# Attention scores from queries and keys stored as rounded halves, stacked to 128 rows

## The reference

```python
proj = rmsnorm(x) @ w_in          # q, k, v of group A and of group B, 512 columns each
# group A: 4 heads of differential attention; 2 parts of q and k with 64 channels, v with 128
qa = partial_rope(rmsnorm(qa), cos, sin);  ka = partial_rope(rmsnorm(ka), cos, sin)
s = einsum('bhcqd,bhckd->bhcqk', q, k) * scale           # rows of 128 queries, keys up to them
p = softmax(where(mask, s, -inf));  w = p[0] - lam * p[1];  o = w @ v
# group B: 8 heads of stick-breaking attention, 64 channels
z = einsum('bhqd,bhkd->bhqk', q, k) * scale
log_keep = where(mask, log_sigmoid(-z), 0);  suffix = reversed cumsum of log_keep
a = where(mask, exp(log_sigmoid(z) + suffix - log_keep), 0);  o = a @ v
```

## Time and profile before

| | us |
|---|---|
| median of 3 runs | 3598.82 (3597.29 to 3598.83) |
| the profiled execution | 3593.81 |
| its span, first to last instruction | 3592.0 |
| PE busy | 3372.0 (94%) |
| DVE busy | 2401.5 (67%) |
| POOL busy | 1655.2 (46%) |
| ACT busy | 1048.7 (29%) |

### The profile page before, as it was taken

One profiled execution on the slowest core, in us unless ns is written; L12 is line 12 of the kernel. 1 busy time (PEld: TensorE's weight loads), 2 busy tenths in 40 slices (PEclk: granted clock), 3 DMA queues, 4 the chain that ended last, 5 costly groups with the idle time before them and its releaser, 6 DMA issues. The chain is left out here.

```text
span 3592.0 us, 45109 instructions
## 1 busy us (share of the span) xinstructions
PE 3372.0 (94%) x17090; PEld 2942.4 (82%) x17090; DVE 2401.5 (67%) x4484; ACT 1048.7 (29%) x1158; POOL 1655.2 (46%) x847
## 2 busy tenths in 40 slices
PE   7998989998899999999999999995899999999998
PEld 5886656666788999999899989995688888888886
DVE  2401658883311788999999999996567666666665
ACT  3221336652211222333333333332112211221120
POOL 2420000001211356555445544565787777877773
PEclk9997877778999999999999999997999999999999
DMA  3132000003221367666666766788887778777874
GB/s 126 70 115 101 24 24 12 12 1 135 80 88 45 137 206 234 206 239 238 236 234 227 241 232 239 251 321 320 308 295 284 289 289 305 283 286 283 310 277 160
DMA packets 252449, 697.16 MB, mean 194 GB/s; under 512 B 20208, under 2 KB 86640, under 8 KB 245104
## 3 DMA queue, kind: packets, MB, share of 16 engines
q1 hardware_dynamic: 178544, 426.35, 33.6%
q0 software_dynamic: 73728, 268.47, 21.1%
HBM read 564.72 MB, written 130.02 MB: 193 GB/s over the span
## 5 line engine op out<-in xcount | busy, mean ns | idle before, releaser
L1150 PE MATMUL hid_ps<-side_hi,u_hi 128*128 128x384 f32 x2048 | 531.3, 340 | 19.8 <-POOL u_lo L836 10.5
L845 POOL DMA_INDIRECT found<-in_u,pick_u x232 | 330.3, 1424 | 425.0 <-DVE found L1081 389.9
L1878 PE MATMUL part<-v_hi,act_hi 128*128 128x512 f32 x1536 | 475.1, 391 | 50.6 <-POOL act_lo L1801 48.8
L1150 PE MATMUL hid_ps<-side_lo,u_hi 128*128 128x384 f32 x2048 | 522.5, 336 | 0.0
L1150 PE MATMUL hid_ps<-side_hi,u_lo 128*128 128x384 f32 x2048 | 522.5, 336 | 0.0
L1878 PE MATMUL part<-v_lo,act_hi 128*128 128x512 f32 x1536 | 474.2, 390 | 0.0
L1878 PE MATMUL part<-v_hi,act_lo 128*128 128x512 f32 x1536 | 473.7, 390 | 0.0
L836 POOL TENSOR_TENSOR u_lo<-u_raw,u_hi 128x1024 fp32r<-128x1024 f32 x128 | 327.5, 2559 | 264.4 <-ACT u_hi L795 263.8
L1817 DVE TENSOR_TENSOR acc<-acc,part 128x1024 f32<-128x1024 f32 x192 | 234.3, 1220 | 307.0 <-PE part L1878 306.9
L1150 PEld LDWEIGHTS hid_ps<-side_hi,u_hi 128*128 128x128 f32 x2048 | 366.8, 189 | 20.5 <-POOL u_lo L836 10.7
L1796 POOL TENSOR_TENSOR v_lo<-v_raw,v_hi 128x2048 fp32r<-128x2048 f32 x64 | 295.8, 4622 | 186.0 <-ACT v_hi L1769 185.4
(11 more groups left out here) (197 smaller groups left out, 5415.5 us busy)
## 6 DMA issues: line engine op xcount, KB each, us to landing
u_raw<-in_uT SPq DMA_DIRECT2D x128, 512.0 KB
v_raw<-in_v SPq DMA_DIRECT2D x64, 1024.0 KB
hid_d<-hid SPq DMA_DIRECT2D x128, 384.0 KB
gate_d<-stage SPq DMA_DIRECT2D x48, 1024.0 KB, 5.6
act_in<-hid_d SPq DMA_DIRECT2D x64, 768.0 KB, 7.6
gate_in<-gate_d SPq DMA_DIRECT2D x32, 1536.0 KB
w_raw<-in_w_in SPq DMA_DIRECT2D x6, 2048.0 KB, 8.3
w_raw<-in_wq SPq DMA_DIRECT2D x4, 2048.0 KB, 8.5
```

Source lines behind the costliest of these rows:

```text
L845: pool.indirect_dma_start(found[:, g], None, u_d, bass.IndirectOffsetOnAxis(ap=pick_u[:, g, n:n + 1], axis=0))\
L1150: mm = pe.matmul(hid_ps[:, s % 2, half, 0:W], w[:, s % 2, ch], x[:, ch, GB * P + half * W:GB * P + (half + 1) * W], start=n == 0, stop=n = ...
L1878: last = pe.matmul(part[:, n % BANKS, cols], a[:, s, j, rows], v[:, s, j, cols], start=j == 0 and m == 0, stop=j == J - 1 and m == 2)
```

## The change

The projection stores q and k as two rounded halves: ACT writes `st_hi` (fp32r), DVE writes `st_lo`, the PSUM value (scaled for q of B) less `st_hi`. Each has two slots; a slot is free when both stores of the use before have landed. v keeps `st` with two slots. The last transposes of q and of k, and the later items of PE, wait for the low halves too.

For each head or part, `attend` loads q's high half to rows 0 to 63 and its low half to rows 64 to 127 of `q_both`, and k's high half to both row halves of `k_hi`, its low half to both of `k_lo`: 12 transfers of 64 rows x 4 KB for a pair of heads, in place of two of 128 rows. A score call is then two fp32r matmuls over 128 rows, `q_both` by `k_hi` and `q_both` by `k_lo`, for each block of columns. In loop B the value matmul takes the 128 columns of both heads of the pair, and the rows of the other head are not read. `soft` and `logw` now share the memory of `prob`.

```diff
...
         sin = sb("sin", [P, TB, ROT])
         spare = sb("spare", [P, 4, TB // 2 * NH * ROT])
         sq = sb("sq", [P, 2, HALF])
-        st = sb("st", [P, 4, HALF])
+        st = sb("st", [P, 2, HALF])
+        st_hi = sb("st_hi", [P, 2, HALF], R)
+        st_lo = sb("st_lo", [P, 2, HALF], R)
         ss = sb("ss", [P, TB])
         rstd = sb("rstd", [P, TB])
         qk_ss = sb("qk_ss", [P, 2, TB, NH])
...
         rot_ok = sem("rot_ok")
         qt_ok = sem("qt_ok")
         st_ok = sem("st_ok")
-        st_out = [sem(f"st_out{n}") for n in range(4)]
+        st_lo_ok = sem("st_lo_ok")
+        v_out = [sem("v_out0"), sem("v_out1")]
+        qk_out = [sem("qk_out0"), sem("qk_out1")]
         block = c.enter_context(nc.Block())
...
             g, k = n // ITEMS, n % ITEMS
             return stores.index(({2: "va", 3: "qb", 4: "kb", 5: "vb"}[g], k)) + 1
+
+        def kind_index(n):
+
+            return sum((w[0] == "v") == (stores[n][0][0] == "v") for w, _ in stores[:n])
         @block.sync
         def _(sp):
...
             def store(n):
                 what, k = stores[n]
+                m = kind_index(n)
+                sp.wait_ge(st_ok, n + 1)
+                if what[0] == "v":
+                    cols = slice(0, HALF) if what == "va" else slice(HALF, D)
+                    sp.dma_start(v_d[k * P:(k + 1) * P, cols], st[:, m % 2]).then_inc(v_out[m % 2], 16)
+                    return
                 cols = slice((k % 2) * HALF, (k % 2) * HALF + HALF)
-                out = {"qa": qT_d[k // 2][:, cols], "ka": kT_d[k // 2][:, cols],
-                       "qb": qT_d[4 + k // 2][:, cols], "kb": kT_d[4 + k // 2][:, cols],
-                       "va": v_d[k * P:(k + 1) * P, 0:HALF], "vb": v_d[k * P:(k + 1) * P, HALF:D]}[what]
-                sp.wait_ge(st_ok, n + 1)
-                sp.dma_start(out, st[:, n % 4]).then_inc(st_out[n % 4], 16)
+                pair = k // 2 + (4 if what[1] == "b" else 0)
+                hi_d, lo_d = (q_hi_d, q_lo_d) if what[0] == "q" else (k_hi_d, k_lo_d)
+                sp.dma_start(hi_d[pair][:, cols], st_hi[:, m % 2].bitcast(F)).then_inc(qk_out[m % 2], 16)
+                sp.wait_ge(st_lo_ok, m + 1)
+                sp.dma_start(lo_d[pair][:, cols], st_lo[:, m % 2].bitcast(F)).then_inc(qk_out[m % 2], 16)
             load_x(0)
             sp.dma_start(gain[:, :], norm_g_d.unsqueeze(0).to_broadcast([P, D])).then_inc(small_in, 16)
...
                 if n == 3 * ITEMS + 5:
                     load_w(5)
                 store(n)
-            for n in range(4):
-                sp.wait_ge(st_out[n], 16 * len(stores) // 4)
+            for n in range(2):
+                sp.wait_ge(v_out[n], 16 * ITEMS)
+                sp.wait_ge(qk_out[n], 32 * 2 * ITEMS)
         @block.gpsimd
         def _(pool):
...
             def out_slot(n):
-                if n >= 4:
-                    act.wait_ge(st_out[n % 4], 16 * (n // 4))
-                return st[:, n % 4]
+                m = kind_index(n)
+                is_v = stores[n][0][0] == "v"
+                if m >= 2:
+                    act.wait_ge((v_out if is_v else qk_out)[m % 2], (16 if is_v else 32) * (m // 2))
+                return (st if is_v else st_hi)[:, m % 2]
             for tb in range(TB + 1):
                 if tb < TB:
...
                 if tb >= 1:
                     low(tb - 1)
             heads = "p b (h d) -> p b h d"
+
+            def store_low(n):
+                what, k = stores[n]
+                m = kind_index(n)
+                if what[1] == "a":
+                    src = tr_ps[:, k // 2 % 2, 4 * (k % 2):4 * (k % 2) + 4].rearrange("p a b -> p (a b)")
+                else:
+                    src = pr_ps[:, k % 4]
+                dve.wait_ge(st_ok, n + 1)
+                dve.scalar_tensor_tensor(out=st_lo[:, m % 2], in0=src, scalar=HD ** -0.5 if what == "qb" else 1.0,
+                                         in1=st_hi[:, m % 2].bitcast(F), op0=ALU.mult,
+                                         op1=ALU.subtract).then_inc(st_lo_ok, 1)
+
+            def store_lows(what):
+                for k in range(ITEMS):
+                    store_low(stores.index((what, k)))
+
             for g in range(2):
                 for k in range(ITEMS):
                     n = ITEMS * g + k
...
                                       ALU.add).then_inc(qss_ok, 1)
                 dve.wait_ge(qss_ok, ITEMS * (g + 1))
                 dve.tensor_scalar(qk_ss[:, g], qk_ss[:, g], 1.0 / HD, EPS, ALU.mult, ALU.add).then_inc(qvar_ok, 1)
+                if g == 1:
+                    store_lows("qa")
                 dve.wait_ge(qrstd_ok, g + 1)
                 flat = qk[:, g].rearrange("p b (h d) -> p (b h) d", d=HD)
                 dve.tensor_tensor(flat, flat, qk_rstd[:, g].rearrange("p b h -> p (b h)").unsqueeze(2)
...
                     dve.wait_ge(rot_mul, m + 1)
                     dve.tensor_tensor(q1, t[0], t[1], ALU.subtract)
                     dve.tensor_tensor(q2, t[2], t[3], ALU.add).then_inc(rot_ok, 1)
+            for what in ("ka", "qb", "kb"):
+                store_lows(what)
         @block.tensor
         def _(pe):
...
                     pe.wait_ge(copied, n - 3)
                 if n >= 4 + 2 * ITEMS:
                     pe.wait_ge(st_ok, stores_until(n - 4))
+                    if (n - 4) // ITEMS in (3, 4):
+                        pe.wait_ge(st_lo_ok, n - 4 - ITEMS + 1)
                 s = g % 2
                 if g in (3, 4):
                     wide = slice((k % 2) * HALF, (k % 2) * HALF + HALF)
...
                     pe.wait_ge(rot_ok, 2 * g)
                     for pair in range(4):
                         n = 4 * (g - 1) + pair
-                        if pair >= 2:
-                            pe.wait_ge(st_ok, STORED_BEFORE[g] + 2 * (pair - 1))
+                        if pair >= 2 or g == 2:
+                            pe.wait_ge(st_lo_ok, ITEMS * (g - 1) + 2 * (pair - 1))
                         for tb in range(TB):
                             last = pe.transpose(tr_ps[:, pair % 2, tb],
                                                 qk[:, g - 1, tb, pair * P:(pair + 1) * P], ident[:, :])
                         last.then_inc(qt_ok, 1)
-
-
-STORED_BEFORE = {1: 0, 2: 16}
 def route(nc, a_hi, a_lo, x_first, ident, x_d, w_out_d, norm_g_d, wq_d, keysT_d, h_d, score_d):
...
         mask_raw = sb("mask_raw", [P, 2, P])
         mask = sb("mask", [P, 2, P], R)
         unit = sb("unit", [P, P], R)
-        qT = sb("qT", [P, 2, T])
-        kT = sb("kT", [P, 2, T])
+        q_both = sb("q_both", [P, 4, T], R)
+        k_hi = sb("k_hi", [P, 4, T], R)
+        k_lo = sb("k_lo", [P, 4, T], R)
         v = sb("v", [P, TB, D])
         prob = sb("prob", [P, 3, 2, T])
-        soft = sb("soft", [P, 2, T])
-        logw = sb("logw", [P, 2, T])
+        soft = prob[:, 0]
+        logw = prob[:, 1]
         ones = sb("ones", [P, T])
         wT = sb("wT", [P, 4, PER, P])
         peak = sb("peak", [P, 4])
...
         @block.sync
         def _(sp):
             def load_pair(n):
-                sp.dma_start(qT[:, n % 2], qT_d[n]).then_inc(qk_in[n % 2], 16)
-                sp.dma_start(kT[:, n % 2], kT_d[n]).then_inc(qk_in[n % 2], 16)
+                for part in range(2):
+                    s = 2 * (n % 2) + part
+                    rows = slice(part * HD, part * HD + HD)
+                    for half, q_d in enumerate((q_hi_d, q_lo_d)):
+                        here = slice(half * HD, half * HD + HD)
+                        sp.dma_start(q_both[here, s].bitcast(F), q_d[n][rows]).then_inc(qk_in[n % 2], 16)
+                        sp.dma_start(k_hi[here, s].bitcast(F), k_hi_d[n][rows]).then_inc(qk_in[n % 2], 16)
+                        sp.dma_start(k_lo[here, s].bitcast(F), k_lo_d[n][rows]).then_inc(qk_in[n % 2], 16)
             load_pair(0)
             sp.dma_start(mask_raw[:, 0], mask_da_d).then_inc(mask_in, 16)
...
         @block.tensor
         def _(pe):
-            def scores(out, rows, buf, i, kind):
-
-                q = qT[rows, buf, i * P:(i + 1) * P]
+            LOADED = 16 * 12
+
+            def scores(out, s, i, kind):
+
+                q = q_both[:, s, i * P:(i + 1) * P]
                 for a, b in spans(i):
-                    pe.matmul(out[:, a:b], q, kT[rows, buf, a:b], start=True, stop=True)
-                pe.matmul(out[:, i * P:(i + 1) * P], q, kT[rows, buf, i * P:(i + 1) * P], start=True, stop=False)
+                    pe.matmul(out[:, a:b], q, k_hi[:, s, a:b], start=True, stop=False)
+                    pe.matmul(out[:, a:b], q, k_lo[:, s, a:b], start=False, stop=True)
+                d = slice(i * P, (i + 1) * P)
+                pe.matmul(out[:, d], q, k_hi[:, s, d], start=True, stop=False)
+                pe.matmul(out[:, d], q, k_lo[:, s, d], start=False, stop=False)
                 return pe.matmul(out[:, i * P:(i + 1) * P], unit[:, :], mask[:, kind], start=False, stop=True)
             def scores_a(u):
```

(15 more changed lines are left out.)

18 lines of the change are left out of this document (12 added, 6 removed).

## The result

The changed kernel takes 3540.15 us (median of 4 runs, 3538.07 to 3542.95) against 3598.06 (3595.53 to 3598.83) for the kernel before on the same chip: ratio 0.9841, 95% interval 0.9824 to 0.9858. Its profiled execution took 3538.5 us with a span of 3536.7. PE's busy time fell from 3372.0 to 3221.9 us. The time, 3540, lies 9 us under the forecast of 3549 and inside its own range.

What follows compares the result with a forecast made beforehand. PE at the lower clock level was taken to set the attention stage's pace, DVE being the next bound. 37 + 34 - 17 - 4 = 50 us off 3593.8 gives 3544, plus 5 for the median 3549; own range 3532 to 3568, overall 3524 to 3588.

Steps and rivals of the forecast that it cites:

- The whole: Whole kernel: 37 + 34 - 17 - 4 = 50 us off the profiled execution's 3593.8, median 3549.
- Score call: Attention scores, upper clock level: 512-column block 0.46 us instead of 0.97, diagonal with mask 0.36 instead of 0.57.
- Loop A: Differential attention, 4 heads: gain 37 us, bounds 28 to 48, out of DVE's 63.7 us wait for scores.
- +6 for v: Loop A: v lands at about 344 instead of 337, so PE stands at its first value matmul, 6 us lost.
- Loop B: Stick-breaking attention, 8 heads: of 52.5 us of DVE waits 18 stay, gain 34 us, bounds 15 and 48.
- value matmuls: Loop B, 64 weight columns become 128 in 576 records: 0 change, bounds -1 and +1 us.
- The clock: Attention loops: stacked matmuls bring the upper level back sooner after each gap; mean clock above 0.8 in both loops.
- Store side: Projection's q and k stores: +17 us (q's transposes +4, k's +10, lower clock +2.5), bounds +6 and +24.
- Start: First loads of attention: 3 MB per pair instead of 1 at 381 GB/s, +4 us, bounds +2 and +12.
- half-rate loads: Rival, new 64-row loads: half of 381 GB/s, first two pairs 16.5 us each, v 16 later: 3565; chance 0.24.
- The clock stays up: Rival, both attention loops: denser matmuls hold 2.4 GHz throughout, time 3522; chance 0.12.
- Slower, the clock stays down: Rival, both attention loops: PE idles more and stays at 1.2 GHz, attention gains nothing, time 3626; chance 0.12.

Runs made afterwards that it cites:

- 64-row mask kernel: Kernel before the change, with only its mask matmul cut from 128 rows to the 64 rows of its call: 3553.28 us, ratio 0.9857.
- The kernel with the side costs mended: Changed kernel with the later weight load, three slots for the halves, first pair and v loaded in halves, pair 1 last: 3508.22 us, ratio 0.9752.

## Why the prediction was right, point by point

- *The whole.* 50 us off the profiled execution were forecast, 55.3 came. The mechanism held: PE stops being the bound, DVE becomes it. That the sum is so near is partly luck: the loops gave 25.0 us more than forecast, the store side, the start and v cost 16.7 more (2.6, 7.2 and 6.9), and 3.0 came on behind the loops, which the forecast had left untouched and no run explains.
- *Score call.* Right in sum, not in its parts. The 512-column pair was taken at 0.46: it takes 385.54 - 385.01 = 0.53 in the call shown, as only its second matmul keeps to 0.23. Diagonal and mask were taken at 0.36 and take 385.01 - 384.68 = 0.33 there, 0.28 in most calls. In the unit with four blocks off the diagonal, at the upper level, the two calls take 1.67 us up to the transposes, 2 x 0.83 for 2 x 0.82 forecast. I did not see that half of the 0.57 of diagonal and mask was the change from 64 to 128 rows and back, which the stacking removes.
- *Loop A.* Forecast -37, of which +6 for v, so -43 without. Measured -45.8 with 12.9 for v, so -58.7 without. The term mis-sized is what is left of the wait for scores: 26 forecast less v's 6 gives 20, and 10.9 stood, 9 of the 15.7 us. DVE's busy time, which the forecast kept, fell from 124.4 to 121.9 between the marks; the rest is in smaller waits. The clock is 0.81, above 0.8 even with 13 us of idle time at 0.50 in it.
- *Loop B.* Forecast -34, measured -43.3. Of 52.5 us of waits I left 18; 10.1 + 2.8 = 12.9 stood. With the values back at 64 columns 13.2 + 4.5 = 17.7 stood, so these 5 us are the value matmuls. The other 4 of the 9.3 are mostly DVE's busy time, 235.3 for 239.0. The term mis-sized is that of the value matmuls, which I had put at 0 with bounds of 1 us either side, from their equal pitch. The pitch inside a group is equal indeed; the change of columns at its two ends is what costs, and bounds taken inside a group could not hold it. The Trainium skill (TensorE: Matmul & The Clock Gate, LDWEIGHTS) would have a load of 128 columns dearer; here the wider loads made the loop faster.
- *The clock.* I expected the stacked matmuls to bring the upper level back sooner, from the first head of A with its 64 rows. It did, from 384.6 us on: 0.91 from 379 to 409. My reason, that head's 64 rows, is not shown. The 64-row mask kernel reaches 0.91 there with 64-row scores, and the unedited loop reached 1.00 there in one of four profiles. It is shown that 128 rows, which leave no border of rows, stand higher in both loops (0.89 and 0.92 for 0.75 and 0.72, with nothing else changed). What of it is the rows and what the borders is not.
- *Store side.* Forecast +17, measured +19.6. q's gap about 3: 3.06, though 5.20 in the second profile; projection matmuls resumed 4.9 later (forecast 4). k's gap 8 to 11: 10.17. k's last transposes came at 198.28 for 181.17, 17.1 later. 4.9 of these are q's. Another 1.8 were lost behind q's gap, where the projection matmuls came every 0.43 us instead of 0.23 from 138.59 to 142.43, which the forecast had only in its bound. The rest is k's. Then 2.5 more were lost until the stage's end, the forecast share of the lower clock.
- *Start.* Forecast +4, measured +11.2: the failed step. It took 381 GB/s from a transfer of 128 rows for transfers of 64; they ran at 212. This is the rival "half-rate loads". It said 16 us for start and v together, and came out at 11.2 - 4 = 7.2 and 12.9 - 6 = 6.9, 14.1 us. Its time of 3565 was missed only because the loops gave 15.7 and 9.3 us more than forecast, which paid for it.
  The Trainium skill (SBUF — State Buffer, Door 1: The DMA port swizzle) has this rule, half of the ports for rows 0 to 63; this trace agrees, with 212 GB/s against 380 for 128 rows.
- *The clock stays up* (3522) did not come: 0.81 and 0.87 are no clock held through both loops. The kernel with the side costs mended reached 3508, but that is no test of it, since the 3522 had these costs in it.
- *Slower, the clock stays down* (3626) did not come. With 64-row rounded matmuls and the 128-row mask the loops stay at 0.74 and 0.70, and even then the time was 3574.

## What to carry to other kernels

Look along PE's order for neighbours of different row or column counts before shortening the matmuls themselves: making them equal, with the same number of matmuls, was worth 2.1% over 128 rows and 1.4% by the mask alone, where the whole change gave 1.6%. When an operand is stored in two parts, list every place where a slot is reused behind a large load on the same queue, and every load that now writes 64 rows; these places held 32 us here. Profile a loop twice before you explain its clock. Bound an edit by what stands at the ends of a group too, not by the pitch inside it.

## What was not expected of the hardware

- A matmul of 128 rows starts 0.20 us after the 64-row one ahead of it, and one of 64 rows 0.26 us after one of 128, where equal counts give 0.11; values of 64 columns between neighbours of 128 cost 0.09 at the one end, and 16 of them with the other end 0.19.
- PE full for 29.93 of 30 us was granted 0.51 with such borders in every call; full for 28.40 of 30 and for 27.14 of 28 without them inside a call, 0.91 both times. But with them it also stood at 1.00 for 22 us in one profile, so what holds the level low stays open.
- Matmuls of the two parts, on different 64 rows and with no 128-row matmul between them, took 2.14 us for two calls, less than the 2.44 of the same calls over 128 rows.
- Transfers to 64 rows, three by three to either half on one queue, moved 212 to 222 GB/s at a full busy share of the DMA engines, transfers to 128 rows 380: those to the two halves gained nothing from each other.
- The same unedited loop A took 216.5 and 201.5 us in two profiles of one kernel, at 0.75 and 0.81.
